# Running sums of a chunked scan, spread over the partitions by one transposed table split into high and low parts instead of one product per head

## The reference

```python
acs = jnp.cumsum((dt * a_neg).reshape(b, nc, q, g, hg), axis=2)      # per chunk of 128 tokens
seg = acs[:, :, :, None] - acs[:, :, None, :]
decay_in = jnp.exp(jnp.where(tri[:, :, None, None], seg, NEG_INF))
cb = jnp.einsum('bctgn,bcsgn->bctsg', cc, bc)
y_diag = jnp.einsum('bctsg,bctsgh,bcsghp->bctghp', cb, decay_in, xdt)
states = jnp.einsum('bcsgn,bcsgh,bcsghp->bcghpn', bc, decay_out, xdt)
...                                                                  # states carried from chunk to chunk
y = y_fwd + y_bwd + d_skip * xs
```

## Time and profile before

| | us |
|---|---|
| median of 3 runs (lowest, highest) | 2820.43 (2819.46, 2824.1) |
| the profiled execution's own time | 2819.14 |
| its span | 2817.4 |
| PE busy | 2667.3 (95%) |
| DVE busy | 1478.6 (52%) |
| ACT busy | 930.6 (33%) |
| POOL busy | 720.9 (26%) |

### The profile page before, as it was taken

The page is one execution under the profiler, slowest core; times in us unless marked ns, Lnnn a source line. Parts: engine busy times, 40 slices in busy tenths (PEclk is TensorE's granted clock), DMA queues, the critical chain, the costliest instruction groups (busy, mean ns, idle before and its releaser), DMA issues.

```text
span 2817.4 us, 35461 instructions
## 1 busy us (share of the span) xinstructions
PE 2667.3 (95%) x13860; PEld 2241.6 (80%) x13860; DVE 1478.6 (52%) x1751; ACT 930.6 (33%) x1454; POOL 720.9 (26%) x388
## 2 busy tenths in 40 slices
PE   5999998899999999999899999898999999999997
PEld 5988987787888888888688799786878888888885
DVE  5366557826444444444465655586464444444443
ACT  3345554513222222222234355453132222222221
POOL 2232110023333333333223301100333333333330
PEclk9999999999999999999999999999999999999998
DMA  5433343121111111111123344521111111111111
GB/s 184 135 99 120 127 146 132 53 75 45 45 45 45 45 48 50 53 45 45 58 90 85 103 129 142 172 83 68 45 45 45 45 45 48 51 52 45 45 45 60
DMA packets 74104, 214.08 MB, mean 76 GB/s; under 512 B 5832, under 2 KB 30408, under 8 KB 72776
## 3 DMA queue, kind: packets, MB, share of 16 engines
q1 hardware_dynamic: 53192, 180.67, 19.9%
q10 hardware_dynamic: 20776, 31.39, 3.3%
HBM read 178.45 MB, written 33.59 MB: 75 GB/s over the span
## 4 chain that ended last, share of the span: by engine, by line
PE 89%; DVE 6%; ACT 2%; issue 2%; DMA 0%; ACTq 0%; DVEq 0%; SPq 0%
PE PS L448 22%; PE PS L451 22%; PE PS L452 21%; PE PS L518 4%; PE PS L522 3%; PE PS L521 3%; PE PS L774 2%; PE PS L672 2%; PE PS L661 2%; PE PS L790 1%; PE PS L651 1%; PE PS L650 1%; PE PS L824 1%; DVE ACC L1238 1%; DVE HL L1259 1%
## 5 line engine op out<-in xcount | busy, mean ns | idle before, releaser
L448 PE MATMUL PS<-HH,WH 128*128 128x512 f32 x1920 | 765.4, 399 | 4.7 <-DVE HL L1638 4.7
L451 PE MATMUL PS<-HL,WH 128*128 128x512 f32 x1920 | 763.6, 398 | 0.0
L452 PE MATMUL PS<-HH,WL 128*128 128x512 f32 x1920 | 763.3, 398 | 0.0
L437 POOL CAST WH<-RAW 128x1024 fp32r<-128x1024 f32 x192 | 235.0, 1224 | 2019.3 <-PE PS L448 1526.5
L439 POOL TENSOR_TENSOR WL<-RAW,WH 128x1024 fp32r<-128x1024 f32 x192 | 491.4, 2559 | 15.4
L1655 DVE TENSOR_TENSOR X<-PS,X 128x512 f32<-128x512 f32 x384 | 259.7, 690 | 398.8 <-PE PS L452 378.5
L448 PEld LDWEIGHTS PS<-HH,WH 128*128 128x128 f32 x1920 | 363.2, 189 | 93.5 <-DVE HL L1638 5.2
L452 PEld LDWEIGHTS PS<-HH,WL 128*128 128x128 f32 x1920 | 363.2, 189 | 88.8
L451 PEld LDWEIGHTS PS<-HL,WH 128*128 128x128 f32 x1920 | 363.4, 189 | 88.0
L1197 ACT ACTIVATE FPAD<-PS 128x512 f32<-128x512 f32 x176 | 103.2, 600 | 886.9 <-PE PS L452 886.7
L1674 DVE SCALAR_TENSOR_TENSOR CVV<-FPAD,PARM,CVV 128x1024 f32<-128x1024 f32 x44 | 87.1, 1980 | 415.8 <-ACT CVV L1203 415.8
(11 more groups left out here) (199 smaller groups left out, 3234.8 us busy)
## 6 DMA issues: line engine op xcount, KB each, us to landing
RAW<-wst SPq DMA_DIRECT2D x192, 512.0 KB, 3.5
TOE<-toe_d SPq DMA_DIRECT2D x64, 512.0 KB, 3.7
XBS<-xbc_d SPq DMA_DIRECT2D x24, 512.0 KB, 4.4
xspill<-X ACTq DMA_DIRECT2D x2, 4096.0 KB, 13.0
xbc_d<-CV ACTq DMA_DIRECT2D x16, 512.0 KB, 3.4
tok_d<-ST ACTq DMA_DIRECT2D x16, 512.0 KB, 3.2
ZG<-tok_d SPq DMA_DIRECT2D x16, 512.0 KB, 3.5
X<-xspill SPq DMA_DIRECT2D x2, 4096.0 KB, 12.1
```

Source lines behind the costliest of these rows:

```text
L437: nc.gpsimd.tensor_copy(hi, RAW[:, hf, :]).then_inc(hi_done, 1)
L448: ins = nc.tensor.matmul(out, wh, xh, start=first, stop=False)
L451: nc.tensor.matmul(out, wh, xl, start=False, stop=False)
L452: return nc.tensor.matmul(out, wl, xh, start=False, stop=last)
```

## The change

The running sums are already there for all chunks in `ACS`, 8 chunks by 16 columns, that is 128 columns. The change turns this table once per layer, with one PE transpose at f = 8 of the column tiles (`decays_turn`), and DVE copies the turned table over the parameter columns `w_dt`, which are no longer needed, between `conv5(2)` and the making of `WST`. Its 128 rows are now chunk by 4 groups by 4 heads, with the tokens along the free axis.

In `far`, DVE then makes `MH` and `ML`, each of 4 blocks of 128 columns. Block h holds the turned table with all rows set to zero except those whose head within the group is h (`fourth`), rounded to float32r in `MH`, and the remainder in `ML`. `SEL` holds 32 columns; column r is one on the four rows of the group r.

`sums` now makes three float32r products of 512 columns: the mask as before, and a column of `SEL`, broadcast over 128 weight columns, with `MH` and with `ML`. The four products per head are gone, and with them `AST`, its copy on ACT and the semaphore between. The constants that are loaded at the start grow from 512 to 548 columns.

```diff
-        CST = place("CST", [P, 4 * P])
+        CST = place("CST", [P, 4 * P + 36])
...
+        fourth, fours = CST[:, 4 * P:4 * P + 4], CST[:, 4 * P + 4:4 * P + 36]
...
-        AST = place("AST", [P, 16], u_at + 19968)
+        SEL = place("SEL", [P, 32], u_at + 19968, F32R)
...
+        MH = place("MH", [P, 4, P], m_at[0], F32R)
+        ML = place("ML", [P, 4, P], m_at[0] + 2048, F32R)
...
+                def decays_turn():
+
+                    pe.wait_ge(acs_ready, l + 1)
+                    nc.tensor.transpose(PS[:, 4, 0:P], ACS[:].rearrange("p c e -> p (c e)"), ident).then_inc(acst_full, 1)
+
-                between = {0: dt_columns, 1: lambda: heads_turn(3), 2: dt_turn, 6: decays}
+                between = {0: dt_columns, 1: lambda: heads_turn(3), 2: dt_turn, 6: decays, 8: decays_turn}
...
                         g, d = divmod(j, 2)
-                        if j == 0:
-                            pe.wait_ge(ast_ready, n + 1)
                         pe.wait_ge(exp_ready, n * 4 + j + 1)
                         nc.tensor.matmul(bank(2 + j % 2), IDR[:, :],
                                          FAR[:, d, :].unsqueeze(1).to_broadcast((P, 4, P)),
                                          start=True, stop=False, skip_group_check=True)
-                        for h in range(4):
-                            e = d * 8 + g * 4 + h
-                            last = nc.tensor.matmul(PS[:, 2 + j % 2, h * P:(h + 1) * P],
-                                                    AST[:, e:e + 1].to_broadcast((P, P)),
-                                                    tri_f if d == 0 else tri_b, start=False, stop=True,
-                                                    skip_group_check=True)
+                        rows = n % NT * 4 + d * 2 + g
+                        for part in (MH, ML):
+                            last = nc.tensor.matmul(bank(2 + j % 2), SEL[:, rows:rows + 1].to_broadcast((P, P)),
+                                                    part[:].rearrange("p h n -> p (h n)"), start=False,
+                                                    stop=part is ML, skip_group_check=True)
                         last.then_inc(ab_full, 1)
...
-                    act.wait_ge(ab_full, 1 + n * 4)
-                    A(AST[:], DTA[:, c, :], ACT.Copy).then_inc(ast_ready, 1)
...
                 conv5(2)
+                dve.wait_ge(acst_full, l + 1)
+                nc.vector.tensor_copy(par_("w_dt"), PS[:, 4, 0:P])
                 dve.wait_ge(dec_ready, l + 1)
...
                     for d, tri in enumerate((tri_f, tri_b)):
-                        last = TS(FAR[:, d, :], tri, 1.0, 1e30, ALU.subtract, ALU.mult)
+                        TS(FAR[:, d, :], tri, 1.0, 1e30, ALU.subtract, ALU.mult)
+                    nc.vector.tensor_copy(SEL[:], fours)
+                    for h in range(4):
+                        last = TS(MH[:, h, :], par_("w_dt"), fourth[:, h:h + 1], None, ALU.mult)
+                    last.then_inc(far_step, 1)
+                    dve.wait_ge(far_step, l + 1)
+                    for h in range(4):
+                        last = STT(ML[:, h, :], par_("w_dt"), fourth[:, h:h + 1], MH[:, h, :].bitcast(F32),
+                                   ALU.mult, ALU.subtract)
                     last.then_inc(far_ready, 1)
```

More of the change, by code:

```diff
@@ L256, in trunk @@
         GT = work("GT", [P, GW])
+        MH = place("MH", [P, 4, P], m_at[0], F32R)
+        ML = place("ML", [P, 4, P], m_at[0] + 2048, F32R)
+        assert m_at[0] + 4096 <= x_at
         PS = ctx.enter_context(nc.psum_tensor("PS", [P, 8, HALF], F32))
@@ L288, in trunk @@
             sem("ra_t_full"), sem("ra_bst"), sem("ra_xw"), sem("ra_s_full"), sem("ra_done"), sem("ra_step"))
-        ast_ready, t_full, bst_ready, xs_ready = sem("ast_ready"), sem("t_full"), sem("bst_ready"), sem("xs_ready")
+        acst_full, far_step = sem("acst_full"), sem("far_step")
+        t_full, bst_ready, xs_ready = sem("t_full"), sem("bst_ready"), sem("xs_ready")
         ab_full, curf_ready, y12_done, gt_done = sem("ab_full"), sem("curf_ready"), sem("y12_done"), sem("gt_done")
@@ L1733, in chip_constants @@
     i = np.arange(P)
-    return np.concatenate([np.eye(P), i[:, None] <= i[None, :], i[:, None] >= i[None, :], np.ones((P, P))],
-                          axis=1).astype(np.float32)
+    return np.concatenate([np.eye(P), i[:, None] <= i[None, :], i[:, None] >= i[None, :], np.ones((P, P)),
+                           i[:, None] % 4 == np.arange(4), i[:, None] // 4 == np.arange(32)], axis=1).astype(np.float32)
 def weight_stream(w_in, w_out, w_up, w_down):
```

## The result

| | before | after |
|---|---|---|
| median (lowest, highest), 4 runs each | 2819.94 (2819.06, 2824.1) | 2771.61 (2769.5, 2775.24) |
| profiled execution's span | 2817.4 | 2768.7 |
| ratio, 95% interval | | 0.9827 [0.981, 0.9844] |

The forecast was 2810.6 us and a gain of 10; the gain is 48.

The account below looks back on a forecast made before the run. PE was taken to bound the kernel, with DVE close behind in the chunk loop. Per layer -6.2 - 0.7 + 1.85 + 0.15 = -4.9 us, -9.8 for both, gave 2810.6 us; range 2806.5 to 2816.5.

Parts of the forecast that it names:

- part 4: Turn at f = 8 and larger constants: transpose with semaphore costs 0.15 us per layer, DVE 0, constants about 0.1 at most.
- the 36 columns more of constants: Load at the start: 7% more of one load, costing about 0.1 us at most.
- The loop: Chunk loop: `sums` 1.13 to 0.72 us, period 11.66 to 10.77, DVE's limit; seven periods gain 6.2 us a layer.
- The margin of 0.15 us: Chunk loop: line 824's result reaches DVE at 6.04 us, before DVE is ready for line 1617 at 6.19.
- another wait: Rival, chunk loop: a new wait leaves the period at 11.0 to 11.2 us; about 2816.8 us, chance 0.12.
- the uncovered float32r weights: Rival, `sums`: products with a broadcast weight column not overlapped, period 12.74 us; 2840 us, chance 0.06 for slower.
- `far`: Backward states, between addition and next `XWA`: added DVE work wholly on the path, 1.85 us per layer, bounds 1.3 to 3.7.
- the clock's fall into the chunk loop: Rival: PE's idling in the loop lowers its clock; two or three falls give 2813 us, chance 0.10.
- the first chunk: Ahead of each layer's first `GT`: `GT` at 453.3 in place of 454.0, a gain of 0.7 us.
- The turn at f = 8: Column tiles: one PE transpose, 0.11 us per layer, 0.15 with its semaphore; DVE's part costs 0.
- the cover: DVE at f = 8: copy, `WST` and `NACS` end at 174.6, taps start at 175.41; 0.8 us left.

Follow-up runs that it names:

- the timeline of step 4 above: Changed kernel with the weight tiles 64 bytes higher and the `far` pieces spread over steps 3 to 6 of the backward states: 2752.7 us, ratio 0.9766.
- the wider constants: Kernel before with only the constants' tile 36 columns wider, never loaded or read, so all behind lies 160 bytes higher: 2781.85 us, ratio 0.9868.
- At the old places: Changed kernel with the 36 columns in a tile of their own at the end, so other tiles keep the addresses of the kernel before: 2812.61 us, ratio 0.9982.
- 96 empty bytes: Kernel before with 96 bytes left free ahead of HH: 2766.99 us, ratio 0.981.
- three tests: Kernel before, 160 bytes ahead of WH: 2816.78 us; changed kernel, EA ahead of weights: 2759.57; kernel before, 32 bytes ahead of WH, 64 of HH: 2807.89.
- AHI and ALO alone: Kernel before with 160 bytes left free ahead of the tiles that begin with KN, QN, AHI, ALO; HH, HL, X stay: 2818.67 us, ratio 0.9999.
- 160 and 96 bytes ahead of HH: Two runs of the kernel before with bytes left free directly ahead of HH: 160 bytes 2781.74 us (0.9862), 96 bytes 2766.99 us (0.981).

## Why the prediction was wrong

**The step that failed** is the last sentence of part 4: that the 36 columns more of constants cost about 0.1 us at most, as 7% of one load. I counted their bytes and not their place. They moved the streamed tiles by 160 bytes against the weights, and this changed the slot of 7872 products that the change doesn't touch, from 234.2 to 228.7 ns. It is 35 to 41 of the 48 us: 2781.85 against 2817.21 by moving the places under the old instructions, 2771.61 against 2812.61 by moving them under the new ones. Nothing in the rows of one kernel could have given the size; but that all addresses behind the constants move, and that two thirds of the chain run at 234 ns a product, both could be read, and belonged into the range.

**The loop** was right: one `sums` 0.70 us (0.72 forecast), the period 10.71 (10.77), DVE without its two waits, the gain 13.3 us for both layers (12.4). The margin of 0.15 us between line 824 and 1617 held. The rivals of another wait and of the uncovered float32r weights didn't come true.

**`far`** was right in its mechanism and near in its size: 2.04 us a layer, 1.85 forecast. The instructions with two tensors went by in 0.26 us each (0.27 forecast). The four scalings with a column of `CST` took 0.20 each from start to start (0.79 us for four in the timeline of step 4 above), not 0.135 as those with constants; the durations of the two kinds:

```profile
L1536 DVE TENSOR_SCALAR FAR<-CST x4: 218/219/220, 429.7 to 1792.0; 128x128 fp32r<-128x128 f32 x4
L1539 DVE TENSOR_SCALAR MH<-PARM,CST x8: 278/279/280, 430.1 to 1792.8; 128x128 fp32r<-128x128 f32 x8
```

That is 0.06 us more for each and 0.24 a layer, where I had counted 0. The Trainium skill (VectorE: DVE Perf Modes, "Mode 2x_2P") names a constant as the other operand, and the prediction gave 0.07 more for each if a column loses the double rate. The size fits this, but a fixed cost of a column operand would fit as well, and no run here tells the two apart.

Missed was what stood behind `far`. I had put the clock's fall into the chunk loop, where it didn't come (1.00 throughout), and not here, where I had worked out myself that PE would stand still. PE idled 3.29 us and the following stretch was granted 0.51. The Trainium skill (TensorE: Matmul & The Clock Gate, "HAM oscillation") describes the same: PE waits between two bursts of products, and the next burst starts at the lower clock.

With this the stage cost 6.3 us for both layers in place of the 2.3 that 1.85 - 0.7 gives. The two steps, 5.05 and 3.57 to 3.63, make 6.1 of them. The rest is the first chunk. From the last step to the first `GT` it took 10.4 us before. In the second layer, at a full clock, it now takes 9.9, a gain of 0.5 where 0.7 was forecast. In the first layer it takes 11.0, since the clock fell there too (PE starts on the first chunk at 443.51):

```profile
443.40:446.80 3.40, 3.29 (x14) 3.06 (x15) 0.54 (x3) 0.72 (x2) 0.00 (x0) 0.54 0.00 0
```

That fall isn't the change's alone: falls come and go in this stage between profiles of unchanged instructions (59.4 us before, 64.0 with the wider constants).

**The turn at f = 8** cost PE nothing that can be seen. On DVE the cover held, but with 0.26 us left in place of the 0.8 I counted, since `NACS` took 1.02 us there, 0.29 before:

```profile
170.96 1.02 DVE L1444 TENSOR_TENSOR NACS<-LDT,ACS 128x128 f32<-128x128 f32 x1
172.23 5.14 DVE L1409 SCALAR_TENSOR_TENSOR CV<-PAD,PARM,CV 128x1024 f32<-128x1024 f32 x2 [0.26 <-ACT CV L1040]
```

At the old places the whole edit is worth 5 us (2 to 8 by the interval) against the 10 forecast; the backward states cost 4 us more than forecast and the loop gave 1 more. The 2812.6 us there would have lain in the range, so the move of the tiles alone took the time out of it, and the error in the backward states would have stayed hidden.

## What to carry to other kernels

Where two kernels differ by a tile's size, all tiles behind it have moved: compare the distance from start to start of a product that the change doesn't touch before giving its gain to the change, and run the old kernel once with only the addresses changed. In a kernel bound by PE, try the offset between the weight tiles and the streamed tiles by itself; here 96 empty bytes were worth 50 us, ten times what the edit gives at the old places. Work put on DVE between two steps of a chain with PE costs its own length and here, with PE idle for 3.29 us, also the clock behind it; cut into pieces it fitted into waits that were there.

## What the runs showed of the hardware

The slot of a float32r product of 512 columns, with a fresh weight tile for each, was 226.6, 228.7, 233.2 or 234.2 ns at a full clock by the distance between the two tiles' addresses; absolute addresses had no effect in three tests. In the traces of four of these kernels (before, AHI and ALO alone, 160 and 96 bytes ahead of HH) the mean slot is the same within 0.2 ns whether DVE, ACT, POOL or a DMA is busy at the time or not. So the traffic of another engine isn't what makes the difference. That PE's own two reads meet in the memory is the nearest explanation, but no run shows it.

The Trainium skill (TensorE: Matmul & The Clock Gate, "Step-by-step: what each phase is for") says that PE's two read ports are independent and that loading the next weights doesn't take bandwidth from the running product. By that the place of one operand against the other should cost nothing; the runs show that it makes 3.3% of a slot (226.6 against 234.2 ns), and the measurement decides.

Open is why AHI and ALO at the same two addresses took 229 ns when HH was at distance 0 or 64 and 232.7 when it was at 160.
